# The final norm of a three-block network: its sums made beside the last product, its last multiplications shared by two engines

## The chip, the cores and the metric

The kernel runs on one core of one Trainium2 chip. The metric is the device time of one execution in microseconds (us), lower is better; the time before is the median of three runs. The engines of the core are TensorE (PE in the profile, its weight loads PEld), VectorE (DVE), ScalarE (ACT), GpSimd (POOL) and SyncE (SP), which here only issues DMAs.

## The reference

Three blocks of different kinds (an RWKV and differential-attention block, a convolution and sparse-attention block, a linear-attention block) work one after the other on a residual stream `x` of 512 tokens by 1024 features. Only the end of the third block is touched by the change:

```python
def rmsnorm_3(x, g):
    x32 = x.astype(jnp.float32)
    y = x32 * lax.rsqrt(jnp.mean(x32 * x32, axis=-1, keepdims=True) + EPS)
    return (y * g.astype(jnp.float32)).astype(x.dtype)

def third_block(...):
    for l in range(DEPTH):
        u = rmsnorm_3(x, g_norm_mix[l])
        x = x + mixer_block(u, ...).astype(x.dtype)
        u = rmsnorm_3(x, g_norm_mlp[l])
        x = x + jnp.square(jax.nn.relu(u @ w_mlp_in[l])) @ w_mlp_out[l]
    return rmsnorm_3(x, g_final)
```

The last line is the final norm: each token's 1024 features are squared and summed, and every feature is multiplied by the reciprocal root of the mean and by its own weight `g_final`.

## The kernel before

Data lies with the features on the 128 partitions: `x` is 8 tiles of 128 features by 512 tokens, tile k holding features 128k to 128k + 127. A sum over features is therefore a matmul with a matrix of ones.

The dense products run in `chain`, one stage that works through a list of `Job`s. A job is a weight matrix cut into slabs of 8 x 128 x 128 weights. SP loads slab s into a ring of four buffers (`wbuf`, the first of which is called `ahead`), ACT copies it to a rounded high part (`whi`, L256), DVE subtracts to get the low part (`wlo`, L338), and PE multiplies high by high, low by high and high by low (L240), 24 matmuls of 128x512 a slab. ACT and DVE make the parts three slabs ahead of PE; a buffer of `whi` is free again when PE has done the slab four before (`w_used`). When a tile of the output is complete, its `evict` takes it out of PSUM. In the last job of the third block, the second half of `mlp_out`, a tile takes two slabs, and the eviction is one DVE addition `x<-acc,x` (L404): 8 tiles, 16 slabs.

The order on each engine is written out by hand in the blocks of `chain`: for slab s first the parts of slab s + 3, then statistics, then the eviction. Some jobs already carry a `Fold`: there the squares (ACT, L271) and their running sum (DVE, L372) of the norm that follows are made right after each tile's eviction, and after the job PE needs one matmul with the ones (`stat`, L216), DVE the mean plus epsilon (L350), ACT the root (L267) and DVE the reciprocal (L359). The last job has no `Fold`.

After `chain` has closed, with a barrier of all engines, a stage of its own, `rmsnorm`, makes the final norm: SP loads the weights (L514), ACT squares the 8 tiles (L529), PE sums them with 8 matmuls into one PSUM bank (L542; float32, so the trace shows 16), DVE the mean (L554), ACT the root (L531), DVE the reciprocal (L556), then 8 multiplications by weight and reciprocal at once (L559), each released to SP, which stores the tile (L521) and at the end waits for all stores. The semaphores of a stage are cleared at its end.

Of the kernel before, what the change touches and what calls it, by code (L numbers as in the profile page):

```python
# [58 lines left out]
class Job:  # L59
# [15 lines left out]
    def makes_pair(self, n):  # L75
        return self.kind in ("join", "relu2") or (self.kind == "ffn" and n % 2 == 1) or self.fold is not None
# [15 lines left out]
class Fold:  # L92
# [3 lines left out]
    def __init__(self, pair, cols, eps, inner=None, eps_inner=None):  # L96
        self.pair, self.cols, self.eps, self.inner, self.eps_inner = pair, cols, eps, inner, eps_inner

# [5 lines left out]
def chain(nc, ones, jobs, T, norm, pending=None, ring=4, side=None, loads=(), taps=None, restore=None, ahead=None,  # L104
# [39 lines left out]
    for s, f in folds:  # L144
        per = 7 * (2 if f.inner is not None else 1)
        sum_no[s], summed_total = (summed_total, summed_total + per), summed_total + per
        fold_job[s] = slabs[s - 1][0]
    two_norms = any(f.inner is not None for f in stat_at.values())
# [11 lines left out]
    with stage(nc) as s_:  # L160
# [18 lines left out]

        first_in = wbuf[0]  # L180
# [10 lines left out]
        with nc.Block() as block:  # L191
            @block.sync
            def _(sp):
# [11 lines left out]
                if following is not None:  # L205
                    sp.wait_ge(lo_ready, (S - 1) // ring * ring + 1)
                    n = following.shape[3] // -(-following.shape[3] // 8)
                    sp.dma_start(first_in[:, 0:n, :], following[0, 0, :, 0:n, :]).then_inc(ahead[1], 16)

            @block.tensor  # L210
            def _(pe):
# [9 lines left out]
                for s, (j, n, i) in enumerate(slabs):  # L221
# [23 lines left out]
                    if side is not None:  # L245
                        side.pe(pe, s, stat)

            @block.scalar
            def _(act):
# [19 lines left out]
                def folded(f, n, x):  # L269
                    copy(f.pair[0][n], x, ACT.Copy, scale=f.cols[:, n:n + 1]).then_inc(hi_done, 1)  # L270
# [57 lines left out]
                if loads:  # L328
                    act.wait_ge(arrived, 16 * len(loads))

            @block.vector
            def _(dve):
# [28 lines left out]
                def folded(f, n, x, last):  # L361
                    no = sum_no[last][0]
                    dve.wait_ge(hi_done, part["made", fold_job[last], n])
# [78 lines left out]
                for s, (j, n, i) in enumerate(slabs):  # L442
# [12 lines left out]
                    if side is not None:  # L455
                        side.dve(dve, s)

# [31 lines left out]


def rmsnorm(nc, ones, x, weight, out, T, eps, src=None, dst=None):

    pair = isinstance(out, tuple)
    K = x.shape[1]
    nh, th = halves(T)
    with stage(nc) as s:
        w = s.sb("norm_w", [P, K])  # L500
        sq = s.sb("squares", [P, K, T])
        rstd = s.sb("rstd", [P, T])
        acc = s.ps("sum_squares", [P, nh, BANK])
        loaded, squared, summed = s.sem("loaded"), s.sem("squared"), s.sem("summed")
        mean_ready, root_ready, order, stored = s.sem("mean_ready"), s.sem("root_ready"), s.sem("order"), s.sem("stored")
        ready, hi_ready = s.sem("normed"), s.sem("hi_ready")

        whole = sq if pair else out
        acc_v = acc[:, :, 0:th]
        rstd_v = rstd[:].rearrange("p (h t) -> p h t", h=nh)  # L510
        with nc.Block() as block:  # L511
            @block.sync
            def _(sp):
                sp.dma_start(w[:], weight).then_inc(loaded, 16)  # L514
                if src is not None:
                    for k in range(K):
                        sp.dma_start(x[:, k, :], src[:, k, :]).then_inc(loaded, 16)
                if dst is not None:
                    for k in range(K):
                        sp.wait_ge(ready, k + 1)  # L520
                        sp.dma_start(dst[:, k, :], out[:, k, :]).then_inc(stored, 16)  # L521
                    sp.wait_ge(stored, 16 * K)

            @block.scalar
            def _(act):
                for k in range(K):
                    if src is not None and k == 0:
                        act.wait_ge(loaded, 16 + 16 * K)
                    nc.scalar.activation(sq[:, k, :], x[:, k, :], ACT.Square).then_inc(squared, 1)  # L529
                act.wait_ge(mean_ready, 1)  # L530
                nc.scalar.activation(rstd[:], rstd[:], ACT.Sqrt).then_inc(root_ready, 1)  # L531
                if pair:
                    for k in range(K):
                        act.wait_ge(ready, k + 1)
                        nc.scalar.activation(out[0][:, k, :], whole[:, k, :], ACT.Copy).then_inc(hi_ready, 1)

            @block.tensor
            def _(pe):
                for k in range(K):
                    pe.wait_ge(squared, k + 1)  # L540
                    for h in range(nh):
                        mm = nc.tensor.matmul(acc[:, h, 0:th], ones[:], sq[:, k, h * th:(h + 1) * th],  # L542
                                              start=(k == 0), stop=(k == K - 1))
                mm.then_inc(summed, 1)

            @block.vector
            def _(dve):
                def low_part(k):
                    dve.wait_ge(hi_ready, k + 1)
                    nc.vector.tensor_tensor(out[1][:, k, :], whole[:, k, :], out[0][:, k, :].bitcast(F32), ALU.subtract)  # L550

                chain = Chain(dve, order)
                dve.wait_ge(summed, 1)
# [3157 lines left out]
```

## Time and profile before

| | us |
|---|---|
| median of 3 runs | 3673.82 |
| the three runs | 3668.71 to 3677.48 |
| span of the profiled execution | 3676.3 |
| PE busy in it | 3363.3 (91%) |
| DVE, ACT, POOL busy | 2025.1, 1230.3, 203.8 |
| HBM read, written | 264.22 MB, 19.89 MB |

The profile lists for one execution what every engine did and when. The span runs from the first to the last instruction, and all times of the trace are counted from its start. "Idle before" is the time an engine stood still before an instruction, with the instruction that ended the wait. PEclk is the clock that TensorE was granted, as a share of full speed.

### The profile page before, as it was taken

The page shows a single profiled execution, that of the slowest core. Times are in us where ns is not written, and L with a number is a line of the kernel's source. Part 1 is how long each engine was busy: PE and PEld are TensorE (multiplying, and loading weights), DVE is VectorE, ACT ScalarE, POOL GpSimd, SP SyncE. Part 2 cuts the span into 40 slices and gives each one's busy share as a digit, 9 for nine tenths or more (in the row PEclk, how much of TensorE's full clock was granted, in tenths as well). Part 3 has the DMA queues.
Part 4 walks back from the last instruction along what each step waited for, and adds up shares of the span by engine and source line. Part 5 has one row for each costly group of instructions (what it writes and reads, how often), then busy time and mean ns, then how long its engine had stood idle before and what let it go on. Part 6 is the DMA issues. An engine that isn't in the chain of part 4 may idle for free. (4 is left out here: it accounts for less than half of the span.)

```text
span 3676.3 us, 57266 instructions
## 1 busy us (share of the span) xinstructions
PE 3363.3 (91%) x24193; PEld 2748.5 (75%) x24193; DVE 2025.1 (55%) x3289; ACT 1230.3 (33%) x2142; POOL 203.8 (6%) x171
## 2 busy tenths in 40 slices
PE   7978999988999999888999998978699889999998
PEld 6868888956888888656677776866578587878886
DVE  4875654565355344577546776356736545464342
ACT  4542332254334233214433222234412234233231
POOL 2213220010000000000000000000100020000000
PEclk9989998988999999989999999989799889999999
DMA  4431103201322222520122222312022003233231
GB/s 147 156 124 48 48 19 116 69 1 52 97 93 92 98 92 80 145 72 13 47 75 92 86 86 93 99 59 93 13 92 95 1 2 109 78 106 98 93 97 58
DMA packets 99462, 287.84 MB, mean 78 GB/s; under 512 B 19738, under 2 KB 23962, under 8 KB 97160
## 3 DMA queue, kind: packets, MB, share of 16 engines
q1 hardware_dynamic: 93104, 269.43, 22.6%
q10 hardware_dynamic: 6104, 14.75, 1.6%
q8 instruction: 193, 3.16, 0.4%
q14 instruction: 61, 0.50, 0.0%
HBM read 264.22 MB, written 19.89 MB: 77 GB/s over the span
## 5 line engine op out<-in xcount | busy, mean ns | idle before, releaser
L240 PE MATMUL acc<-h_hi,whi 128*128 128x512 f32 x1992 | 800.5, 402 | 65.4 <-DVE wlo L432 43.0
L240 PE MATMUL acc<-h_hi,wlo 128*128 128x512 f32 x1992 | 791.1, 397 | 0.0
L240 PE MATMUL acc<-h_lo,whi 128*128 128x512 f32 x1928 | 770.0, 399 | 0.0
L240 PEld LDWEIGHTS acc<-h_hi,whi 128*128 128x128 f32 x1992 | 379.1, 190 | 176.0 <-DVE wlo L432 45.3
L338 DVE TENSOR_TENSOR wlo<-wbuf,whi 128x1024 fp32r<-128x1024 f32 (+3 forms) x277 | 318.6, 1150 | 272.9 <-ACT whi L256 270.5
L240 PEld LDWEIGHTS acc<-h_hi,wlo 128*128 128x128 f32 x1992 | 379.3, 190 | 87.8
L240 PEld LDWEIGHTS acc<-h_lo,whi 128*128 128x128 f32 x1928 | 366.8, 190 | 86.2 <-issue 2.9
L256 ACT ACTIVATE whi<-wbuf 128x1024 fp32r<-128x1024 f32 (+3 forms) x277 | 274.5, 991 | 347.4 <-PE acc L240 318.3
L240 PE MATMUL acc<-arena_round,whi 128*128 128x512 f32 x736 | 236.6, 392 | 4.8 <-DVE arena_round L398 4.8
L338 DVE TENSOR_TENSOR wlo<-ahead,whi 128x1024 fp32r<-128x1024 f32 (+3 forms) x132 | 152.3, 1154 | 140.9 <-ACT whi L256 140.2
L256 ACT ACTIVATE whi<-ahead 128x1024 fp32r<-128x1024 f32 (+3 forms) x132 | 131.4, 995 | 174.7 <-PE acc L240 168.3
L240 PEld LDWEIGHTS acc<-arena_round,whi 128*128 128x128 f32 x736 | 139.2, 189 | 35.0 <-DVE arena_round L398 5.6
L240 PE MATMUL acc<-arena_round,wlo 128*128 128x512 f32 x416 | 162.8, 391 | 0.0
L240 PE MATMUL acc<-gates_round,whi 128*128 128x512 f32 x384 | 141.2, 395 | 3.0 <-DVE gates_round L398 1.8
L404 DVE TENSOR_TENSOR x<-acc,x 128x512 f32<-128x512 f32 x64 | 44.3, 692 | 178.1 <-PE acc L240 178.1
L670 PE MATMUL acc<-h_hi,whi 128*128 128x264 f32 x432 | 127.4, 295 | 7.5 <-POOL wlo L658 7.5
L240 PE MATMUL acc<-gates_round,wlo 128*128 128x512 f32 x320 | 125.5, 392 | 0.0
L670 PE MATMUL acc<-h_hi,wlo 128*128 128x264 f32 x432 | 123.5, 286 | 0.0
L670 PE MATMUL acc<-h_lo,whi 128*128 128x264 f32 x432 | 123.5, 286 | 0.0
L1430 PE MATMUL acc<-h_hi,whi 128*128 128x264 f32 x384 | 115.9, 302 | 1.1 <-DVE wlo L1468 1.1
L289 ACT ACTIVATE val<-tmp 128x512 f32<-128x512 f32 x64 | 40.5, 633 | 216.7 <-DVE tmp L400 216.7
L1430 PE MATMUL acc<-h_lo,whi 128*128 128x264 f32 x384 | 109.6, 285 | 0.0
(748 smaller groups left out, 6265.7 us busy)
## 6 DMA issues: line engine op xcount, KB each, us to landing
wbuf<-in_mlp_out SPq DMA_DIRECT2D x46, 512.0 KB, 3.3
wbuf<-in_mlp_in SPq DMA_DIRECT2D x45, 512.0 KB, 3.3
wbuf<-in_w_gates SPq DMA_DIRECT2D x38, 512.0 KB, 3.4
wbuf<-in_ffn_up SPq DMA_DIRECT2D x29, 512.0 KB, 3.3
wbuf<-in_w_qkv SPq DMA_DIRECT2D x23, 512.0 KB, 3.4
rwkv_factors<-factors SPq DMA_DIRECT2D x8, 1320.0 KB, 4.6
ahead<-in_mlp_in SPq DMA_DIRECT2D x19, 512.0 KB, 3.4
wbuf<-in_w_rwkv SPq DMA_DIRECT2D x18, 512.0 KB, 5.7
```

What stands on the lines that cost most here:

```text
L240: mm = nc.tensor.matmul(acc[t % NB][:, 0:T], wt[s % ring][:, k - a, :], xt, start=(kx == 0 and q == 0), stop=(kx == job.K - 1 and q == 2))
L256: copy(whi[s % ring][:, 0:size(s), :], wbuf[s % ring][:, 0:size(s), :], ACT.Copy).then_inc(hi_ready, 1)
L289: copy(val[t % 2][:], tmp[t % 2][:], ACT.Square)
L338: TT(wlo[s % ring][:, 0:size(s), :], wbuf[s % ring][:, 0:size(s), :], whi[s % ring][:, 0:size(s), :].bitcast(F32), ALU.subtract).then_inc( ...
L404: TT(job.dst[n], ps, job.other[n], ALU.add).then_inc(evicted_d, 1)
L670: mm = nc.tensor.matmul(acc[n % 2][:, hf, 0:H], wt[n % R][:, kx, :], xt[:, kx, at], start=(kx == 0 and q == 0), stop=(kx == 7 and q == 2))
L1430: mm = nc.tensor.matmul(acc[n % NB][:, h, 0:H], wt[n % R][:, k, :], xt[:, k, h * H:(h + 1) * H], start=(k == 0 and q == 0), stop=(k == 7 a ...
```

## The change

The stage `rmsnorm` and its call are dropped. The last job gets a new kind of fold, `Ending`, that holds the columns of the final weight (a ninth column block of the resident tile `norms`, which grows from 256 to 288 bytes a partition), epsilon and the output.

- While the last product runs, ACT squares each tile of `x` after its eviction and then multiplies the tile in place by its weight; DVE adds the square to the running sum.
- After the last tile PE makes one matmul of the sum with the ones, DVE the mean plus epsilon, ACT the root, DVE the reciprocal, all inside `chain`.
- The multiplications by the reciprocal are now plain products of two tiles. DVE makes tiles 0, 1, 2, 4, 5 and 7, GpSimd tiles 3 and 6, each after waiting for the reciprocal.
- SP stores the tiles in the order 0 to 7, each after the product that makes it.

```diff
--- before.py
+++ after.py
@@ -73,7 +73,7 @@
         return self.kind in ("copy", "sigmoid") and not self.scaled
 
     def makes_pair(self, n):
-        return self.kind in ("join", "relu2") or (self.kind == "ffn" and n % 2 == 1) or self.fold is not None
+        return self.kind in ("join", "relu2") or (self.kind == "ffn" and n % 2 == 1) or isinstance(self.fold, Fold)
 
 
 class Ahead:
@@ -95,6 +95,13 @@
 
     def __init__(self, pair, cols, eps, inner=None, eps_inner=None):
         self.pair, self.cols, self.eps, self.inner, self.eps_inner = pair, cols, eps, inner, eps_inner
+
+
+class Ending:
+
+
+    def __init__(self, cols, eps, dst):
+        self.cols, self.eps, self.dst, self.inner = cols, eps, dst, None
 
 
 def tile_list(ap):
@@ -145,6 +152,9 @@
         per = 7 * (2 if f.inner is not None else 1)
         sum_no[s], summed_total = (summed_total, summed_total + per), summed_total + per
         fold_job[s] = slabs[s - 1][0]
+    ending = next((f for _, f in folds if isinstance(f, Ending)), None)
+    ends_on = jobs[-1].dst
+    by_dve_last = (0, 1, 2, 4, 5, 7)
     two_norms = any(f.inner is not None for f in stat_at.values())
 
     def first_tile(j):
@@ -177,6 +187,8 @@
             s_.sem(n) for n in ("stat_ready", "var_ready", "root_ready", "scale_ready", "inverse_ready", "inner_ready", "order", "padded",
                                 "conv_done", "gelu_done", "arrived"))
 
+        scaled, last_normed, last_stored = (s_.sem(n) for n in ("scaled", "last_normed", "last_stored")) if ending else (None,) * 3
+        last_pool = s_.sem("last_pool") if ending else None
         first_in = wbuf[0]
         if side is not None:
             side.prepare(s_, evicted_d)
@@ -206,6 +218,22 @@
                     sp.wait_ge(lo_ready, (S - 1) // ring * ring + 1)
                     n = following.shape[3] // -(-following.shape[3] // 8)
                     sp.dma_start(first_in[:, 0:n, :], following[0, 0, :, 0:n, :]).then_inc(ahead[1], 16)
+                if ending is not None:
+                    for k in range(8):
+                        if k in by_dve_last:
+                            sp.wait_ge(last_normed, by_dve_last.index(k) + 1)
+                        else:
+                            sp.wait_ge(last_pool, 1 if k == 3 else 2)
+                        sp.dma_start(ending.dst[:, k, :], ends_on[k]).then_inc(last_stored, 16)
+                    sp.wait_ge(last_stored, 16 * 8)
+
+            @block.gpsimd
+            def _(pool):
+                if ending is not None:
+                    pool.wait_ge(scale_ready, len(stat_at) + 1)
+                    pool.wait_ge(scaled, 8)
+                    for k in (3, 6):
+                        nc.gpsimd.tensor_tensor(ends_on[k], ends_on[k], scale[:], ALU.mult).then_inc(last_pool, 1)
 
             @block.tensor
             def _(pe):
@@ -244,6 +272,9 @@
                         statistics(s)
                     if side is not None:
                         side.pe(pe, s, stat)
+                if ending is not None:
+                    pe.wait_ge(summed, sum_no[S][1])
+                    nc.tensor.matmul(stat[0][:, 0:T], ones[:], sums[0][:], start=True, stop=True).then_inc(stat_ready, 1)
 
             @block.scalar
             def _(act):
@@ -267,6 +298,10 @@
                     copy(scale[:], scale[:], ACT.Sqrt).then_inc(root_ready, 1)
 
                 def folded(f, n, x):
+                    if f is ending:
+                        copy(sums[0][:] if n == 0 else sqx[n % 2][:], x, ACT.Square).then_inc(sq_done, 1)
+                        copy(x, x, ACT.Copy, scale=f.cols[:, n:n + 1]).then_inc(scaled, 1)
+                        return
                     copy(f.pair[0][n], x, ACT.Copy, scale=f.cols[:, n:n + 1]).then_inc(hi_done, 1)
                     copy(sums[0][:] if n == 0 else sqx[0][:], x, ACT.Square).then_inc(sq_done, 1)
                     if f.inner is not None:
@@ -327,6 +362,9 @@
                         side.act(act, s)
                 if loads:
                     act.wait_ge(arrived, 16 * len(loads))
+                if ending is not None:
+                    act.wait_ge(var_ready, len(stat_at) + 1)
+                    copy(scale[:], scale[:], ACT.Sqrt).then_inc(root_ready, 1)
 
             @block.vector
             def _(dve):
@@ -360,6 +398,13 @@
 
                 def folded(f, n, x, last):
                     no = sum_no[last][0]
+                    if f is ending:
+                        dve.wait_ge(sq_done, no * 8 // 7 + n + 1)
+                        if n > 0:
+                            if n > 1:
+                                dve.wait_ge(summed, no + n - 1)
+                            TT(sums[0][:], sums[0][:], sqx[n % 2][:], ALU.add).then_inc(summed, 1)
+                        return
                     dve.wait_ge(hi_done, part["made", fold_job[last], n])
                     STT(out=f.pair[1][n], in0=x, scalar=f.cols[:, n:n + 1], in1=f.pair[0][n].bitcast(F32), op0=ALU.mult,
                         op1=ALU.subtract).then_inc(lo_done, 1)
@@ -454,6 +499,16 @@
                         STT(out=x[s - 1], in0=x[s - 1], scalar=cols[:, s - 1:s], in1=inner_rstd[:], op0=ALU.mult, op1=ALU.mult)
                     if side is not None:
                         side.dve(dve, s)
+                if ending is not None:
+                    no = len(stat_at) + 1
+                    dve.wait_ge(stat_ready, no)
+                    TS(scale[:], stat[0][:, 0:T], 1.0 / (8 * P), ending.eps, ALU.mult, ALU.add).then_inc(var_ready, 1)
+                    dve.wait_ge(root_ready, no)
+                    nc.vector.reciprocal(scale[:], scale[:]).then_inc(scale_ready, 1)
+                    dve.wait_ge(scale_ready, no)
+                    dve.wait_ge(scaled, 8)
+                    for k in by_dve_last:
+                        TT(ends_on[k], ends_on[k], scale[:], ALU.mult).then_inc(last_normed, 1)
 
 
 def settle(eng, sem):
@@ -486,82 +541,6 @@
                 for dst, src in pairs:
                     sp.dma_start(dst, src).then_inc(arrived, 16)
                 sp.wait_ge(arrived, 16 * len(pairs))
-
-
-def rmsnorm(nc, ones, x, weight, out, T, eps, src=None, dst=None):
...
-                    nc.scalar.activation(sq[:, k, :], x[:, k, :], ACT.Square).then_inc(squared, 1)
...
-                        mm = nc.tensor.matmul(acc[:, h, 0:th], ones[:], sq[:, k, h * th:(h + 1) * th],
...
-                    nc.vector.scalar_tensor_tensor(out=whole[:, k, :], in0=x[:, k, :], scalar=w[:, k:k + 1], in1=rstd[:],
...
 T1 = 528
@@ -3510,12 +3489,10 @@
                 Job(a["up_3"][1], pairs[1], "sum", dst=arena[8:16], gate=arena[8:16], other=arena[16:24], raw=parts[1]),
                 Job(a["up_3"][0], pairs[0], "join", dst=joined, gate=arena[0:8], other=arena[8:16], raw=parts[0]),
                 Job(a["w_out_3"], joined, "add", dst=xs, other=xs, source=3, fold=Fold(now, norms[:, MLP[1], :], 1e-6))]
-        jobs += mlp_jobs(xs, now, hidden, a["mlp_in_3"], a["mlp_out_3"], None)
+        jobs += mlp_jobs(xs, now, hidden, a["mlp_in_3"], a["mlp_out_3"], Ending(norms[:, LAST, :], 1e-6, out))
         for j, source in ((5, 4), (6, 5), (8, 7)):
             jobs[j].source = source
         chain(nc, ones, jobs, T2, norm, ahead=ahead.take(), side=HeadNorm(nc, ones, o_m, a["norm_mlstm_3"], norm[1][1], norm[2]))
-    rmsnorm(nc, ones_ident["ones"], x, a["norm_final_3"], x, T2, 1e-6, dst=out)
-
 
 def program(nc, a, out):
 
@@ -3540,7 +3517,7 @@
 
 
 
-INNER, OUTER, MLP, FFN, PLE = (0, 2), (1, 3), (4, 5), 6, 7
+INNER, OUTER, MLP, FFN, PLE, LAST = (0, 2), (1, 3), (4, 5), 6, 7, 8
 CONSTANTS = {
     0: ["ones", "ident", "norms"],
     1: ["blk64", "mean64", "chunk_start1", "causal_pair", "level_pair", "eye_pair", "mask128", "rope_cos", "rope_sin", "rope_swap"],
@@ -3688,7 +3665,7 @@
         a[name] = column(i[key])
     a["norms"] = np.stack([column(v) for v in (
         i["final_norm_w"], i["norm_mix_2"], i["norm_final_2"], i["g_norm_mix_3"], i["norm_mlp_w"][0], i["g_norm_mlp_3"], i["norm_ffn_2"],
-        i["norm_ple_2"])], 1)
+        i["norm_ple_2"], i["g_final_3"])], 1)
     a["up_3"] = np.stack([tiles(i["w_up_3"][0, n], 4) for n in range(3)])
     a["w_out_3"], a["mlp_in_3"], a["mlp_out_3"] = tiles(i["w_out_3"][0]), tiles(i["w_mlp_in_3"][0]), tiles(i["w_mlp_out_3"][0])
     return a
```

On DVE, at the end of the program. Before (`rstd` is the reciprocal root, `squares` and `sum_squares` belong to the dropped stage):

```order
L338 TENSOR_TENSOR wlo<-wbuf,whi 128x1024
L404 TENSOR_TENSOR x<-acc,x 128x512 x2
L191 UNCONDITIONAL_BRANCH
L546 UNCONDITIONAL_BRANCH
L554 TENSOR_SCALAR rstd<-sum_squares 128x512
L556 RECIPROCAL rstd<-rstd 128x512
L559 SCALAR_TENSOR_TENSOR x<-x,norm_w,rstd 128x512 x8
```

After, on the same engine at the same place:

```order
L376 TENSOR_TENSOR wlo<-wbuf,whi 128x1024
L449 TENSOR_TENSOR x<-acc,x 128x512
L406 TENSOR_TENSOR sums<-sums,sqx 128x512
L449 TENSOR_TENSOR x<-acc,x 128x512
L406 TENSOR_TENSOR sums<-sums,sqx 128x512
L505 TENSOR_SCALAR scale<-stat 128x512
L507 RECIPROCAL scale<-scale 128x512
L511 TENSOR_TENSOR x<-x,scale 128x512 x6
```

Behind each eviction now stands an addition to the sum, the branch into a stage of its own is gone, and six products of two tiles stand where eight products with weight and reciprocal stood.

On ACT, at the end of the program. Before:

```order
L256 ACTIVATE whi<-ahead 128x1024
L256 ACTIVATE whi<-wbuf 128x1024 x3
L191 UNCONDITIONAL_BRANCH
L524 UNCONDITIONAL_BRANCH
L529 ACTIVATE squares<-x 128x512 x8
L531 ACTIVATE rstd<-rstd 128x512
```

After:

```order
L287 ACTIVATE whi<-wbuf 128x1024 x2
L302 ACTIVATE sqx<-x 128x512
L303 ACTIVATE x<-x,norms 128x512
L287 ACTIVATE whi<-wbuf 128x1024
L302 ACTIVATE sqx<-x 128x512
L303 ACTIVATE x<-x,norms 128x512
L302 ACTIVATE sqx<-x 128x512
L303 ACTIVATE x<-x,norms 128x512
L367 ACTIVATE scale<-scale 128x512
```

The squares moved from behind the barrier to between the parts of the last slabs, each followed by the multiplication by the weight; no load of a function table stands in either stretch. On GpSimd, whose last work before was hundreds of us earlier, the products are new, the last but one row of this piece (before, only the first three of its rows stood there):

```order
L3195 TENSOR_TENSOR sums<-inner_rstd,dec 128x512
L2995 UNCONDITIONAL_BRANCH
L41 ISA
L230 UNCONDITIONAL_BRANCH
L236 TENSOR_TENSOR x<-x,scale 128x512 x2
L203 UNCONDITIONAL_BRANCH
```

These are the products for tiles 3 and 6, beside the six of DVE.

## Rows read from the trace of the kernel before

**Rows 1.** The page, busy time of each engine in the whole span.

```profile
PE 3363.3 (91%) x24193; PEld 2748.5 (75%) x24193; DVE 2025.1 (55%) x3289; ACT 1230.3 (33%) x2142; POOL 203.8 (6%) x171
```

**Rows 2.** Chain that ended last, in time order: start us, length us, what.

```profile
3653.58 0.64 ACT squares L529
...
3654.26 8.85 PE sum_squares L542 x16
...
3663.13 0.70 DVE rstd L554
...
3663.86 0.64 ACT rstd L531
...
3664.52 3.36 DVE rstd L556
...
3667.91 0.75 DVE x L559
```

**Rows 3.** Timeline of DVE, last eviction: start, length, line, operation, [idle before].

```profile
3651.94 0.69 DVE L404 TENSOR_TENSOR x<-acc,x 128x512 f32<-128x512 f32 x1 [10.19 <-PE acc L240]
```

**Rows 4.** Timeline around a `Fold` in the same chain, DVE and PE.

```profile
3301.11 0.68 DVE L372 TENSOR_TENSOR sums<-sums,sqx 128x512 f32<-128x512 f32 x1
...
3304.09 0.42 PEld L216 LDWEIGHTS stat<-sums,ones 128*128 128x128 f32 x2
3304.32 1.02 PE L216 MATMUL stat<-sums,ones 128*128 128x512 f32 x2
```

**Rows 5.** Busy time by stretch: A:B, us, each engine, PEclk, DMA share, GB/s.

```profile
3260.00:3303.00 43.00, 43.00 (x185) 35.32 (x184) 24.73 (x30) 18.54 (x25) 0.00 (x0) 0.97 0.29 98
...
3600.00:3651.90 51.90, 51.90 (x229) 42.63 (x228) 10.12 (x10) 6.37 (x6) 0.00 (x0) 1.00 0.09 31
```

**Rows 6.** The same view, stretches of PE's idle time and the sums.

```profile
3651.90:3654.20 2.30, 0.00 (x1) 0.00 (x0) 0.69 (x1) 0.62 (x2) 0.00 (x0) 1.00 0.00 0
...
3655.30:3658.70 3.40, 3.40 (x6) 1.34 (x5) 0.00 (x0) 2.54 (x5) 0.00 (x0) 0.50 0.00 0
```

**Rows 7.** Timeline of DVE early in the program, two places.

```profile
103.43 2.96 DVE L798 SCALAR_TENSOR_TENSOR k<-dif,vec,rkv 128x528 f32<-128x528 f32 x1
...
198.29 0.77 DVE L798 SCALAR_TENSOR_TENSOR k<-dif,vec,rkv 128x528 f32<-128x528 f32 x1
199.09 2.51 DVE L805 TENSOR_SCALAR kk<-k,vec 128x528 f32<-128x528 f32 x1
```

**Rows 8.** Timeline of GpSimd at the same two places.

```profile
103.44 2.38 POOL L658 TENSOR_TENSOR wlo<-wbuf,whi 128x1024 fp32r<-128x1024 f32 x1 [4.33 <-ACT whi L735]
...
198.37 2.93 POOL L658 TENSOR_TENSOR wlo<-wbuf,whi 128x1024 fp32r<-128x1024 f32 x1 [4.32 <-ACT whi L735]
```

**Rows 9.** Groups of GpSimd's operations by form: count, busy us, mean ns, idle before.

```profile
L1730 POOL TENSOR_TENSOR rot<-p,rope_cos 128x512 f32<-128x512 f32 x8 | 10.2, 1273 | 278.9 <-POOLq L42 195.2 <-PE ps_s L1626 83.8
...
L3216 POOL TENSOR_TENSOR sums<-inner_rstd,dec 128x512 f32<-128x512 f32 x4 | 4.2, 1049 | 8.8 <-DVE inner_rstd L3294 8.8
```

**Rows 10.** Timeline of the last stage: multiplications and store issues.

```profile
3667.91 5.39 DVE L559 SCALAR_TENSOR_TENSOR x<-x,norm_w,rstd 128x512 f32<-128x512 f32 x8
3668.68 4.97 SPq L521 DMA_DIRECT2D out_features<-x  x8
```

**Rows 11.** Busy time by stretch, columns as in Rows 5, while the stores run.

```profile
3669.00:3670.00 1.00, 0.00 (x0) 0.00 (x0) 1.00 (x3) 0.00 (x0) 0.00 (x0) 0.50 0.47 176
3670.00:3671.00 1.00, 0.00 (x0) 0.00 (x0) 1.00 (x2) 0.00 (x0) 0.00 (x0) 0.50 1.04 393
...
3674.00:3675.00 1.00, 0.00 (x0) 0.00 (x0) 0.00 (x0) 0.00 (x0) 0.00 (x0) 0.50 0.92 352
3675.00:3676.30 1.30, 0.00 (x0) 0.00 (x0) 0.00 (x0) 0.00 (x0) 0.00 (x0) 0.50 0.00 0
```

**Rows 12.** Waits by pair over the whole span: us in total, times, longest.

```profile
ACT whi L735 <- DMA first<-in_w_rwkv: 9.0, 5, 2.5
...
ACT whi L303 <- DMA ahead<-in_w_gates: 4.7, 1, 4.7
```

More of the change, by code:

```diff
@@ L488, in _ @@
                 sp.wait_ge(arrived, 16 * len(pairs))
-def rmsnorm(nc, ones, x, weight, out, T, eps, src=None, dst=None):
[L496 to L528, printed above, removed]
-                    nc.scalar.activation(sq[:, k, :], x[:, k, :], ACT.Square).then_inc(squared, 1)
[L530 to L541, printed above, removed]
-                        mm = nc.tensor.matmul(acc[:, h, 0:th], ones[:], sq[:, k, h * th:(h + 1) * th],
[L543 to L553, printed above, removed]
-                nc.vector.tensor_scalar(rstd_v, acc_v, 1.0 / (K * P), eps, ALU.mult, ALU.add).then_inc(mean_ready, 1)
-                dve.wait_ge(root_ready, 1)
-                chain(nc.vector.reciprocal(rstd[:], rstd[:]))
-                dve.wait_ge(loaded, 16 if src is None else 16 + 16 * K)
-                for k in range(K):
-                    nc.vector.scalar_tensor_tensor(out=whole[:, k, :], in0=x[:, k, :], scalar=w[:, k:k + 1], in1=rstd[:],
-                                                   op0=ALU.mult, op1=ALU.mult).then_inc(ready, 1)
-                    if pair and k > 0:
-                        low_part(k - 1)
-                if pair:
-                    low_part(K - 1)
```

## The prediction

> **What bounds the kernel now.** The change touches the last 110 us of the program and one constant at its start, so I read the end of the trace first. The busy shares say that TensorE bounds the whole, with 91% of the span [rows 1]. The stretches say it more sharply for the last product: PE is busy 51.90 of 51.90 us up to its last matmul, at full granted clock, while DVE is busy 10.12 and ACT 6.37 us [rows 5]. What follows is the opposite. The chain of waits from there on is one string of single instructions that hand over to each other [rows 2]. It begins with the last addition `x<-acc,x`, which ends at 3651.94 + 0.69 = 3652.63 [rows 3], and its links are: 0.95 us until the new stage's first square starts at 3653.58, the squares and the 16 matmul passes that follow each other to 3663.11, the mean 0.70, the root 0.64, the reciprocal 3.36, and the first multiplication at 3667.91. The string from the last addition to that point is 3667.91 - 3652.63 = 15.28 us long. Then eight multiplications (5.39 us, to 3673.30) release eight stores of 256 KB, the first issued at 3668.68 [rows 10], and the span ends at 3676.3. So there are two pieces to cost: the string of 15.28 us, and the 8.39 us from the first multiplication to the end.
>
> **Work moved under the product: nothing.** Per tile ACT gains a square and a scaled copy, two instructions of 0.64 us or a little less, 8 x 1.28 = 10 us in 87 us of product; DVE gains seven additions of 0.68 us [rows 2, 4]. What could it delay? ACT waits for the eviction before it makes the next high part, so that part, which stands at the end of the slab before, starts some 0.69 + 1.28 = 2 us later, and the low part on DVE behind it. But both are needed only three slabs later, and the last product spends 10.9 us on two slabs (the additions before it stand that far apart: the last one's idle time is 10.19 us, and 0.69 us busy [rows 3]), so 16 us of slack cover 2. The same pattern already stands in the job `w_out_3`, whose tiles come twice as often and whose fold is longer: in the window 3260 to 3303 PE was busy 43.00 of 43.00 us beside 24.73 us of DVE and 18.54 of ACT [rows 5]. If that cover failed, each late slab would show as idle time of PE. No SP transfer is delayed, since SP waits only for low parts. The dropped load of `norm_w` was on no one's path.
>
> **The string of 15.28 us becomes 7.5.** After the last addition there now stand one square 0.64, one addition to the sum 0.68, the two passes of one matmul, the mean 0.70, the root 0.64 and the reciprocal 3.36 [rows 2, 4]. The matmul, from its first weight load at 3304.09 to the end of its passes at 3304.32 + 1.02 = 3305.34, is 1.25 us [rows 4]. The sum is 7.27 us. The seven handovers cost about 0.03 us each (the mean ends at 3663.83, the root starts at 3663.86 [rows 2]), 0.25 in all: 7.52 us. **Saved: 15.28 - 7.52 = 7.76 us.** One term has two ends. PE stands idle here for 2 us before the matmul, as it did before the first of the old sums (2.30 us without PE work); from 3655.30 to 3658.70 the granted clock was 0.50, which is the 1.2 GHz level, before it came back to 1.00 [rows 6]. At the time of the new matmul, 2.1 to 3.4 us after the last slab, the clock was still 1.00 in that execution, so I take 1.25 us; if the fall comes earlier, both passes run at half the clock and it is up to 0.85 us more.
>
> **The multiplications: do two engines share them?** Split without friction, DVE would make six at a pitch of 5.39 / 8 = 0.67 us, 4.05 us, and GpSimd two. The prices on GpSimd are 1.27 us (two tiles read) and 1.05 us (a tile times a repeated column) [rows 9]; I take 1.27, the form being that of the product here, so 2.5 us beside DVE. But the trace shows what happens when the two work at once. At 103.44 GpSimd starts a subtraction of 2.38 us; DVE's operation of two SBUF tiles starts at 103.43 and takes 2.96 us, where the same line takes 0.77 at 198.29: it ends 0.57 us after GpSimd. At 198.37 GpSimd starts while DVE holds on until 199.06; GpSimd then takes 2.93 instead of 2.38, and DVE's next, started at 199.09, takes 2.51 and ends 0.30 us after GpSimd's [rows 7, 8]. So the two exclude each other, each waits for the other's running instruction, and the waiting GpSimd gets in between two of DVE's. Here both operands of both engines lie in SBUF. The Trainium skill says the same of it (SBUF — State Buffer, the section on its two separate sides): a DVE operation with two SBUF inputs and a GpSimd operation that reads SBUF share a pair of ports as an exclusive lock. The trace agrees, as just shown. Then the eight products take turns. Counting from the reciprocal: tile 0 to 0.69; tile 3 on GpSimd to 1.96; tile 1 to 2.53 (0.57 behind GpSimd); tile 6 to 3.80; tile 2 to 4.37; tiles 4, 5, 7 to 6.38 at 0.67 each. That is 1.0 us longer than the 5.39 of now.
>
> **The stores make it dearer.** Once running, they fill the DMA engines: share 1.04 from 3670 on, 0.92 up to 3675, then nothing [rows 11]. 2.1 MB in about 5.4 us is 0.67 us a tile, just DVE's pace today. They begin some 0.8 us after the first issue (0.47 of the slice 3669 to 3670 is busy [rows 11]) and end at 7.0 us after the first multiplication began. So no split can bring the end closer by making products faster: a frictionless one gains under 0.1 us. A delayed one loses, because SP issues in the order 0 to 7 and tile 2 waits: tile 0 issued at 0.71, tile 1 at 2.55, tile 2 at 4.39, then 3 to 7 to 6.43 (an issue is about 0.35 us). Tiles 2 to 7 are six transfers that start at 4.39 + 0.8 = 5.19 and need 6 x 0.67 = 4.03: the last ends at 9.22 instead of 6.97. **Lost: 2.25 us.** If GpSimd keeps its turn for both products, tile 1 is issued at 3.8 and seven transfers end at 9.3 (lost 2.4); if DVE keeps its turn through all six, tile 3 is issued at 5.3 and tile 7 at 7.0, and the end is 9.5 (lost 2.5). At GpSimd's cheaper price the loss is 1.8. From the last transfer to the end of the span nothing changes: the wait, the barrier, the clearing.
>
> **Sum.** -7.76 + 2.25 = -5.5 us. Span 3676.3 - 5.5 = 3670.8; the profiled execution lies 2.5 us over the median and inside the spread of the three runs, and I carry the difference over: 3673.82 - 5.5 = **3668.3 us**, 0.15% faster. What a measurement of this kernel can tell from no change is about 0.2%, 7.3 us. Own range of this case, with the clock's 0.85 and the prices above: 5.9 to 4.4 us faster.
>
> **Rivals.** *No exclusion at the end* (the products are short and DVE wins nothing by waiting): then the stores set the pace as now and the gain is 7.76 + 0.06 = 7.8 us, 3666.0, just over 0.2%. Against it: at both places of rows 7 and 8 an instruction is held, three in all, among them one of DVE that reads a single tile. *The cover fails*: the later high and low parts reach PE late and part of the gain comes back as gaps in PE between 3565 and 3652; at 2 us a tile on eight tiles it would be 16 us, 3684. It decides only where the delay of 2 us passes the slack of 16, which rows 5 speak against. *The tiles lie elsewhere*, the slower case: `norms` grows by 32 bytes, and every tile allocated behind it starts 32 bytes later, for the whole program. If transfers became longer by it, it would cost where an engine waits for a DMA: the eight pairs in the list of waits, from 9.0 down to 4.7 us, sum to 56 us [rows 12]. To turn 5.5 us of gain into 7.3 of loss, those waits would have to grow by 12.8 us, 23%, which is where this case decides: 3681.1. Against it: `x` is already read at a start of 64 bytes plus k times 2,112, off any round grid for most tiles, and its stores still keep up with DVE's 0.67 us [rows 10, 11]. The Trainium skill gives a rule for it (DMA: Bandwidth & Descriptors, How a descriptor splits into AXI transactions): a transfer that does not start on a multiple of 256 bytes needs an extra transaction, nine instead of eight for a run of 2,048 bytes; by that page's figure the estimate would be an eighth of 56 us, 7 us, and 3675.3. No row here shows such a difference.
>
> **Chances.** The forecast (exclusion, parts covered) 0.78. No exclusion 0.12. The cover fails 0.03. Tiles elsewhere with a visible cost 0.07, a third of it past the point for slower. The runs of before lie 8.8 us apart, so a median of a few moves by 2 or 3 us: of the forecast, a quarter is measured as faster by over 0.2%, and hardly any as slower; of no exclusion, over half. Together: faster 0.27, within 0.2% 0.67, slower 0.06. The range for 8 in 10, with that spread about the forecast and the no-exclusion case inside: 3662.5 to 3674.5.
>
> **What would show it.** Right: PE without a gap up to its last matmul; from the last addition's end to the first product of `x` and `scale` 7.5 us; GpSimd's products or DVE's next to them drawn out (a DVE row of about 1.9 us in the group whose others take 0.69), the last product ending 6.4 us after the reciprocal, stores issued with holes behind tiles 0 and 1, and the span's end about 10.6 us after the first product. Wrong: all DVE products at 0.67 and the end at 8.4 us (no exclusion); gaps in PE inside the last product; the program's earlier stages a few us longer (the shift); a weight load and matmul of `stat` of 2 us (the clock).

## The result and the profile after

The changed kernel took 3668.19 us, the median of 20 runs (3661.17 to 3678.92), against 3674.82 us for the kernel before in its 20 runs beside it (3667.85 to 3682.47). The ratio is 0.9982, 95% interval 0.9975 to 0.9989, that is 4.0 to 9.2 us faster. The forecast was 3668.3 us; against 3673.82, a gain of 5.5 us. The measured gain, 0.18%, stays below the 0.2% from which the forecast would have called the kernel faster.

The page of the profiled execution after, span and busy time (answers to [rows 1]):

```profile
span 3664.6 us, 57236 instructions
...
PE 3351.7 (91%) x24179; PEld 2743.7 (75%) x24179; DVE 2037.6 (56%) x3294; ACT 1235.5 (34%) x2150; POOL 206.7 (6%) x173
```

The end of the chain that ended last, in order of time (start us, length us, what; answers to [rows 2, 3]):

```profile
3645.93 0.70 DVE x L449
3646.65 0.64 ACT sqx L302
3647.32 0.70 DVE sums L406
3648.06 1.14 PE stat L277 x2
3649.23 0.70 DVE scale L505
3649.95 0.64 ACT scale L367
3650.61 3.37 DVE scale L507
3654.00 0.69 DVE x L511
3654.69 1.67 DVEq L203
3656.36 3.48 DVE x L511 x4
```

`DVEq` is DVE's queue: for these 1.67 us DVE's second product was waiting or at work behind its first.

The last addition ends at 3645.93 + 0.69 = 3646.62 and the first product starts at 3654.00: 7.38 us where 15.28 us were before.

The timeline of the last stretch, DVE, GpSimd and the store issues (answers to [rows 10]):

```profile
3654.00 5.84 DVE L511 TENSOR_TENSOR x<-x,scale 128x512 f32<-128x512 f32 x6
3654.04 3.44 POOL L236 TENSOR_TENSOR x<-x,scale 128x512 f32<-128x512 f32 x2 [637.38 <-DVE scale L507]
3654.72 6.43 SPq L227 DMA_DIRECT2D out_features<-x  x8
```

From the first product to the end of the span it is 3664.6 - 3654.00 = 10.6 us, where 8.4 us were before. Narrow windows on the same timeline show single instructions of the two engines:

```profile
3656.28 1.75 DVE L511 TENSOR_TENSOR x<-x,scale 128x512 f32<-128x512 f32 x1
...
3654.04 1.77 POOL L236 TENSOR_TENSOR x<-x,scale 128x512 f32<-128x512 f32 x1 [637.38 <-DVE scale L507]
...
3655.77 1.71 POOL L236 TENSOR_TENSOR x<-x,scale 128x512 f32<-128x512 f32 x1
...
3658.06 0.33 SPq L227 DMA_DIRECT2D out_features<-x  x1
```

GpSimd starts 0.04 us behind DVE's first product and must wait for its end at 3654.69; its own end at 3655.81 lets DVE finish its second at 3656.36, and so on: DVE, GpSimd, DVE, GpSimd, and then four products of DVE. Six products take 5.84 us. The last line is the issue of tile 2's store, 4.06 us after the first product began. The occupation of the DMA engines between 3654 and 3665, 40 slices of 0.275 us in tenths, shows what this does to the stores:

```profile
DMA  0000029920019920019999999999999980000000
```

The first tile goes out alone, then a hole, the second, a hole, and only from 3658.9 on six tiles without a gap until 3663.0.

The last product in two stretches, up to its last matmul, and the stretch that holds the single matmul (A:B, us, each engine's busy time, PEclk, DMA share, GB/s; answer to [rows 5, 6]):

```profile
3560.00:3600.00 40.00, 40.00 (x178) 33.10 (x177) 13.96 (x14) 12.49 (x16) 0.00 (x0) 1.00 0.26 92
3600.00:3645.90 45.90, 45.89 (x203) 37.68 (x201) 11.66 (x13) 9.95 (x13) 0.00 (x0) 1.00 0.07 24
...
3648.00:3649.20 1.20, 1.12 (x2) 0.30 (x2) 0.01 (x1) 0.00 (x0) 0.00 (x0) 1.00 0.00 0
```

PE has no visible gap (0.01 us in 85.90) beside the moved squares and additions, and the matmul ran at full granted clock.

The two profiled spans differ by 11.7 us, and only 23.67 - 17.98 = 5.69 us of that lie behind the last addition (before: 3676.3 - 3652.63; after: 3664.6 - 3646.62). The other 6.0 us lie ahead of it, where the programs differ only in the places of the tiles and in the work moved under the last product, beside which PE has no gap. They are taken up with the experiments.

### The profile page after: what moved, and what is told of

Read it like the earlier page. It is cut to its first block and busy times, and to the rows that moved or that the text cites. A ratio compares the mean times of both kernels' runs of the same rounds, so it can differ in the third digit from the quotient of the medians.

```text
span 3664.6 us, 57236 instructions
## 1 busy us (share of the span) xinstructions
PE 3351.7 (91%) x24179; PEld 2743.7 (75%) x24179; DVE 2037.6 (56%) x3294; ACT 1235.5 (34%) x2150; POOL 206.7 (6%) x173
```

## The experiments

The kernels of one group ran on the same chip beside the kernel before. "String" is the time from the end of the last addition `x<-acc,x` to the first product with the reciprocal, "end" the time from that product's start to the end of the span, both from the profile. Ratios are to the kernel before of the same group.

| kernel | string us | end us | ratio | 95% interval |
|---|---|---|---|---|
| before | 15.28 | 8.4 | 1 | |
| changed | 7.38 | 10.6 | 0.9982 | 0.9975 to 0.9989 |
| after_again | 7.39 | 10.6 | 0.9993 | 0.9982 to 1.0005 |
| all_dve | 7.38 | 8.6 | 0.9978 | 0.9968 to 0.9988 |
| split_alone | 15.27 | 10.3 | 1.0015 | 1.0003 to 1.0027 |
| shift_alone | 15.27 | 8.5 | 1.0006 | 0.9998 to 1.0015 |
| stores_free | 7.38 | 8.6 | 0.9974 | 0.9962 to 0.9986 |
| heavy_cover | 7.38 | 10.6 | 0.9976 | 0.9965 to 0.9986 |
| last_square_pe | 6.72 | 8.6 | 0.9962 | 0.9948 to 0.9976 |
| shorter_tail | 3.34 | 8.7 | 0.9959 | 0.9944 to 0.9974 |
| pool_after_dve | 7.38 | 11.0 | one run | |
| after_third | 7.38 | 10.6 | 0.9980 | 0.9969 to 0.9991 |
| shorter_tail_again | 3.34 | 8.6 | 0.9970 | 0.9959 to 0.9981 |

**The split taken away.** All eight products on DVE:

```diff
-    by_dve_last = (0, 1, 2, 4, 5, 7)
+    by_dve_last = tuple(range(8))
...
-                    for k in (3, 6):
-                        nc.gpsimd.tensor_tensor(ends_on[k], ends_on[k], scale[:], ALU.mult).then_inc(last_pool, 1)
+                pass
```

> The changed kernel with all eight last products on DVE and none on GpSimd. Theory (the two engines exclude each other, and the stores need 0.67 us a tile in any case): the eight products take 8 x 0.67 = 5.4 us instead of 5.84, the stores start without holes, and from the first product to the end of the span it is 8.4 us instead of 10.6. So 2.2 us faster than the changed kernel and 7.7 us faster than before, ratio to before about 0.9979. Rival (the split is worth something, the holes in the stores have another cause): the end comes no earlier or later than 10.6 us after the first product.

The products took less than expected, 4.91 us at a pitch of 0.60, and the end 8.6 us, 2.0 less than in the changed kernel. The interval of the ratio holds the expected 0.9979. The ratio of its partner on the chip, the changed kernel once more, is higher, though the two intervals overlap a little; the 2.0 us are read from the traces:

> The changed kernel unaltered, as the partner of the three others on this chip. Exclusion theory: from the end of the last addition to the first product of x and scale 7.4 us, from there to the end of the span 10.6 us, GpSimd's two products 1.7 to 1.8 us each and two of DVE's about 1.75 us, as in its first profile. Ratio to the kernel before 0.998 to 0.9985, 5 to 7 us. If the first measurement was luck of the run, the ratio is nearer to 1.

Timeline of all_dve, last stretch:

```profile
3660.45 4.91 DVE L507 TENSOR_TENSOR x<-x,scale 128x512 f32<-128x512 f32 x8
3661.17 4.54 SPq L227 DMA_DIRECT2D out_features<-x  x8
```

Eight products on one engine end sooner (4.91 us) than six beside two on the other (5.84 us).

**The split alone.** The kernel before, with the last multiplications divided as in the change, its own stage kept:

```diff
                     nc.scalar.activation(sq[:, k, :], x[:, k, :], ACT.Square).then_inc(squared, 1)
+                if dst is not None:
+                    act.wait_ge(loaded, 16)
+                    for k in range(K):
+                        nc.scalar.activation(x[:, k, :], x[:, k, :], ACT.Copy, scale=w[:, k:k + 1]).then_inc(weighted, 1)
...
+                    for k in (3, 6):
+                        nc.gpsimd.tensor_tensor(x[:, k, :], x[:, k, :], rstd[:], ALU.mult).then_inc(by_pool, 1)
...
+                    for k in on_dve:
+                        nc.vector.tensor_tensor(x[:, k, :], x[:, k, :], rstd[:], ALU.mult).then_inc(ready, 1)
```

> The kernel before with its own last stage kept, and in it only the last multiplications changed: ACT multiplies the tiles by the weight after the squares, hidden behind the sums on PE, then DVE makes the products of tiles 0, 1, 2, 4, 5, 7 and GpSimd those of 3 and 6. Theory: the exclusion is a property of the two engines and the string in front of the products stays 15.3 us, so from the first product to the end of the span 10.6 us instead of 8.4, and the kernel is 2.2 us slower than before, ratio 1.0006. Rival (the split itself helps and only its neighbourhood in the changed kernel spoils it): 8.4 us or less, 7 us in the best case.

Timeline of split_alone, last stretch:

```profile
3674.66 5.83 DVE L578 TENSOR_TENSOR x<-x,rstd 128x512 f32<-128x512 f32 x6
3674.70 3.44 POOL L535 TENSOR_TENSOR x<-x,rstd 128x512 f32<-128x512 f32 x2 [645.14 <-DVE rstd L574]
```

The same 5.83 and 3.44 us in other surroundings, the string unchanged, and the ratio is 1.0015 (1.0006 expected, inside the interval): the only kernel whose interval lies wholly above 1. The end was 10.3 us, 1.95 more than before.

**The two engines made to work one after the other.**

```diff
                     pool.wait_ge(scaled, 8)
+                    pool.wait_ge(last_normed, 6)
```

> The changed kernel, but GpSimd begins its two products only when DVE has made all of its six, so that the two never work at once; nothing else changes, the stores keep their order 0 to 7. Theory (exclusion): DVE's six products take 6 x 0.60 + 0.08 = 3.7 us with none drawn out, GpSimd's two about 1.1 us each, and tiles 3 to 7 are stored late, so the end comes 9.5 to 10.5 us after the first product, no better than 10.6 by much. Rival (DVE's long products have another cause than GpSimd): two of them still take 1.75 us.

Its timeline:

```profile
3655.34 3.70 DVE L512 TENSOR_TENSOR x<-x,scale 128x512 f32<-128x512 f32 x6
3656.06 6.85 SPq L227 DMA_DIRECT2D out_features<-x  x8
3659.22 2.48 POOL L237 TENSOR_TENSOR x<-x,scale 128x512 f32<-128x512 f32 x2 [641.23 <-DVEq L203]
```

No product of DVE is drawn out any more, six take 3.70 us, and GpSimd's take 1.26 us each. So what drew two of DVE's products out to 1.75 us was the wait for GpSimd. The end, 11.0 us, was later than the 9.5 to 10.5 expected. GpSimd began 0.2 us behind DVE's last product, and its first took 1.26 us where 1.1 had been reckoned, so tile 3 was issued at 5.2 us after the first product. From there it is the stores' pace: 0.8 us to the first transfer, five transfers in 3.4 us, and 1.5 us to the end of the span.

**What the stores allow.** As all_dve, but seven of the eight products left out, so that all stores may go at once:

```diff
-                    for k in by_dve_last:
+                    for k in (0,):
...
-                        if k in by_dve_last:
-                            sp.wait_ge(last_normed, by_dve_last.index(k) + 1)
-                        else:
-                            sp.wait_ge(last_pool, 1 if k == 3 else 2)
+                        sp.wait_ge(last_normed, 1)
```

> As all_dve, but DVE makes only the product of tile 0, and the stores of all eight tiles wait for that one alone; the products of tiles 1 to 7 with the reciprocal are left out. Theory (the stores need 0.67 us a tile whatever the engines do): from the first product to the end of the span still 8.4 to 8.6 us as in all_dve, although the multiplying takes 0.7 us instead of 4.9. Rival (the end follows the last product): 8.6 - 4.2 = 4.4 us.

Timeline of stores_free from the product on, and the occupation of its DMA engines between 3650 and 3664 (0.35 us a slice):

```profile
3654.56 0.69 DVE L504 TENSOR_TENSOR x<-x,scale 128x512 f32<-128x512 f32 x1
3655.28 4.48 SPq L224 DMA_DIRECT2D out_features<-x  x8
...
DMA  0000000000000000059999999999999992000000
GB/s 0 0 0 0 0 0 0 0 0 0 0 0 0 0 0 0 0 187 386 375 392 369 386 375 386 363 398 369 404 369 404 375 374 82 0 0 0 0 0 0
```

With 0.69 us of multiplying instead of 4.91 the end is the same 8.6 us, and the transfers fill 5.4 us at some 380 GB/s. The floor of this stretch is the stores, given that the first of them goes out behind the first product.

**The cover made heavier.**

```diff
+                        for spare in (*val, *tmp) if n < 7 else ():
+                            copy(spare[:], x, ACT.Square)
                         copy(sums[0][:] if n == 0 else sqx[n % 2][:], x, ACT.Square).then_inc(sq_done, 1)
```

> The changed kernel with the work hidden under the last product made heavier: beside each of the first seven tiles' squares ACT makes four more that nobody reads, 4 x 0.53 = 2.1 us a tile and 15 us in all. Theory (16 us of slack for each high part): PE stays without a gap up to its last matmul, and the ratio is that of the changed kernel, 0.998 to 0.999; from the end of the last addition on nothing changes, 7.4 and 10.6 us. Rival (the cover is thin): gaps on PE in the last product, up to 15 us, ratio up to 1.002.

Busy time of heavy_cover in the whole last product:

```profile
3565.00:3650.00 85.00, 85.00 (x376) 70.38 (x375) 25.61 (x27) 36.81 (x56) 0.00 (x0) 1.00 0.16 56
```

PE was busy 85.00 of 85.00 us beside 36.81 us of ACT. The ratio, 0.9976, is even below the expected band, but its interval reaches to 0.9986. Ahead of the next high part ACT and DVE now have about 4 us of new work instead of 2. The cover holds that; the rest of the 16 us of slack was not tried.

**The shift of the tiles alone.** The kernel before with the ninth block of columns in `norms` and nothing else:

```diff
-        i["norm_ple_2"])], 1)
+        i["norm_ple_2"], i["g_final_3"])], 1)
```

> The kernel before with nothing changed but the constant norms, which gets its ninth block of columns, so that every tile allocated behind it starts 32 bytes later. Theory: no change, ratio 1.0000 within the interval, and the last stretch from the end of the last addition to the end of the span 23.7 us as before. Rival (the places of the tiles matter; they explain that the first profile of the changed kernel reached its last matmul 6 us earlier than the profile of before): a ratio of about 0.9984 with 6 us gained ahead of the last product, or, the other way, a loss.

The ratio is 1.0006 with 1 in its interval, and the profile's last addition ended at 3651.56 + 0.69 = 3652.25, 0.4 us from the 3652.63 of before. No gain from the places is seen. A loss of up to 0.15% is not excluded; the 7 us that the prediction estimated for this rival would be 1.0019, outside the interval. A third set of runs of the changed kernel was made for the same question:

> The changed kernel unaltered once more, since its two ratios so far, 0.9982 and 0.9993, have intervals that barely meet. By the trace of its last stretch the gain is 23.7 - 18.0 = 5.7 us, 0.9984. If something ahead of the last product also became faster, the ratio would be lower than that in all three.

It gave 0.9980, the expected 0.9984 well inside. The three executions of the changed program that were profiled tell where 6 us ahead of the last product come from. Span and mean granted TensorE clock of changed, after_again and after_third:

```profile
core 0: 3664.6 us, clock 0.951
...
core 0: 3677.2 us, clock 0.948
...
core 0: 3668.9 us, clock 0.950
```

The same program ends 12.6 us later in one execution than in another, all of it ahead of the last addition (string and end are the same to 0.02 and 0.1 us), and its granted clock is lower where it is longer. How much of the 12.6 us that is can be added up from the stretches ahead of the last addition in which the trace shows a granted clock of 0.50: 344.7 us in changed, 368.6 us in after_again. Where PE is the bound, half of such time is lost, so 23.9 us more of it are 12.0 us by this estimate. The same sum settles the 6.0 us of the first pair: before had 355.0 us at 0.50, 10.3 more than changed, which is 5.2 of the 6.0 us. Taken off in this way (end of the last addition less half of the time at 0.50), before, shift_alone and split_alone come to 3475.1, 3473.1 and 3475.1 us, and changed, after_again and after_third to 3474.2, 3474.9 and 3476.9 us. So the 6.0 us come mainly from the granted clock of the two executions, and beyond the 4 us by which these sums differ among themselves neither the tiles' places nor the moved work shows ahead of the last addition. Why the clock differs from one execution to the next stays open.

**A shorter end.** Two further edits on top of all_dve. First the last square goes straight to PE, which has begun with the sum of the other seven:

```diff
-                    pe.wait_ge(summed, sum_no[S][1])
-                    nc.tensor.matmul(stat[0][:, 0:T], ones[:], sums[0][:], start=True, stop=True).then_inc(stat_ready, 1)
+                    pe.wait_ge(summed, sum_no[S][1] - 1)
+                    nc.tensor.matmul(stat[0][:, 0:T], ones[:], sums[0][:], start=True, stop=False)
+                    pe.wait_ge(sq_done, sum_no[S][0] * 8 // 7 + 8)
+                    nc.tensor.matmul(stat[0][:, 0:T], ones[:], sqx[1][:], start=False, stop=True).then_inc(stat_ready, 1)
...
-                        if n > 0:
+                        if 0 < n < 7:
```

> As all_dve, and the last tile's square no longer goes through DVE's addition: PE multiplies the sum of seven tiles with the ones while the last square is still being made, and then adds the last square in the same PSUM bank. Theory: from the end of the last addition to the first product 7.4 - 0.7 = 6.7 us, the rest as in all_dve, 8.6 us; 8.4 us faster than before, ratio about 0.9977. Rival (PE's first matmul comes late or at half the clock and the second queues behind it): 7.4 us or more.

The string was 6.72 us, as expected. The ratio, 0.9962, is lower than the 0.9977 of the trace, which lies just outside its interval (0.9948 to 0.9976). All four kernels of this group have ratios 0.0005 to 0.0015 below what their traces give, against the same runs of the kernel before; why was not found, and the traces are taken for the size of each gain. Second, ACT makes the inverse root at once and the reciprocal goes:

```diff
-                    copy(scale[:], scale[:], ACT.Sqrt).then_inc(root_ready, 1)
+                    copy(scale[:], scale[:], ACT.Abs_reciprocal_sqrt).then_inc(root_ready, 1)
...
-                    nc.vector.reciprocal(scale[:], scale[:]).then_inc(scale_ready, 1)
-                    dve.wait_ge(scale_ready, no)
```

> As last_square_pe, and ACT makes the inverse root in one instruction in place of the root on ACT and the reciprocal of 3.36 us on DVE; its function table is loaded behind the last scaled copy, before the mean is there. Theory: from the end of the last addition to the first product 6.7 - 3.4 = 3.3 us, from there to the end of the span 8.6 us; 23.7 - 11.9 = 11.8 us faster than before, ratio about 0.9968. Rival (the load of the table, 1.28 us, is not hidden): 4.6 us and 0.9971.

Timeline of shorter_tail behind the last addition:

```profile
3646.33 1.12 PE L275 MATMUL stat<-sqx,ones 128*128 128x512 f32 x2 [0.59 <-ACT sqx L300]
3646.91 1.28 ACT L365 ACT_TABLE_LOAD   x1
3647.56 0.69 DVE L503 TENSOR_SCALAR scale<-stat 128x512 f32<-128x512 f32 x1 [1.95 <-PE stat L275]
3648.29 0.63 ACT L365 ACTIVATE scale<-scale 128x512 f32<-128x512 f32 x1
3648.95 4.90 DVE L507 TENSOR_TENSOR x<-x,scale 128x512 f32<-128x512 f32 x8 [0.69 <-ACT scale L365]
```

The load of the function table ends at 3648.19, just before the mean at 3648.25: hidden by 0.06 us. The string is 3.34 us, and string and end together 12.0 us, against 23.7 before and 18.0 in the change. A second set of runs stood beside after_third:

> The kernel shorter_tail unaltered once more, beside the changed kernel on one chip. By the traces of the last stretch it is 18.0 - 12.0 = 6.0 us faster than the changed kernel and 11.7 us faster than before, ratio 0.9968. A ratio of 0.996 again would point to a gain outside the last stretch.

0.9970 against 0.9980 of the changed kernel on that chip: the order is the expected one, though the intervals overlap. The trace supports 11.7 us over the kernel before, 0.9968, and both intervals hold it. This version is faster than before in both sets; over the change the gain is shown by the traces, while the medians alone don't separate the two beyond doubt.

## Why the prediction was right

**Work moved under the product, forecast nothing: right.** PE was busy 45.89 of 45.90 us, and with 15 us more on ACT it still had no gap (heavy_cover).

**The string, forecast 7.52 us: measured 7.38.** The matmul took 1.14 us from its first weight load instead of 1.25 (its two weight loads 0.30 instead of 0.42); the rest agrees row by row. Seven handovers of 0.03 us are 0.21 and not 0.25, so the forecast's own terms sum to 7.48, and less the 0.11 of the matmul that is 7.37. The granted clock stood at 1.00 during the matmul, the end of the term that had been chosen.

**The exclusion, forecast as alternating turns: right in mechanism and order, its size somewhat too large.** The last product ended 5.84 us after the first began, against 6.38. Two terms were mis-sized: the pitch of DVE's plain products is 0.60 us, not the 0.67 taken from the products with a weight [rows 10], and a GpSimd product in its turn holds DVE for 1.1 us (3654.69 to 3655.81), not 1.27; alone it takes 1.26 (pool_after_dve), so some of it overlaps with the wait. split_alone shows the same numbers without any other part of the change, and pool_after_dve shows them vanish when the engines don't meet.

**The stores, forecast 2.25 us lost: measured 10.6 - 8.4 = 2.2.** This agreement is partly luck. The store of tile 2 was released at 4.06 us after the first product instead of 4.39, which by the forecast's own sum should have given 0.3 us less. But the six transfers began 0.84 us behind it and took 4.12 us instead of 4.03, and behind the last transfer the changed kernel needs longer: its transfers end at 3663.0 and the span at 3664.6, 1.6 us, where it was 1.4 before (3674.9 to 3676.3). The forecast's "nothing changes" behind the last transfer was wrong by that 0.2 us. It isn't the split that costs it: all_dve and stores_free, which end in `chain` too, have 1.6 us there, while split_alone and shift_alone, which kept the old stage, have 1.4, and split_alone lost 1.95 us with the same pattern of products. So the 0.2 us go with the end of `chain` in place of the end of `rmsnorm`; which part of it was not tried. That the stores are the floor is shown by stores_free.

How much the turns cost hangs on SP's fixed order too. GpSimd had tile 3 ready at 1.81 us after the first product and tile 6 at 3.48, and the stores of both waited for tile 2. An estimate from these rows (0.84 us from issue to transfer, 0.67 us a tile): stored as they become ready, in the order 0, 3, 1, 6, 2, 4, 5, 7, the last transfer would end at 7.7 us instead of 9.0, and 1.3 of the 2.2 us would be gone. No run tried it.

**Sum.** -7.90 + 2.2 = -5.7 us by the traces, against -5.5 forecast. That the absolute 3668.3 us were met to 0.1 us is luck: the kernel before measured 3674.82 and not 3673.82 beside the change, the medians moved by 6.6 us and not 5.5, and single runs lie 18 us apart. The change came out within 0.2%, the outcome to which the forecast gave 0.67, and the three ratios of the changed kernel, 0.9982, 0.9993 and 0.9980, lie around the 0.9984 that the trace gives.

**The rivals.** No exclusion: refuted by the two drawn-out products of DVE. Its price was right, though: all_dve, where the engines don't meet, is at 0.9978, and 7.8 us faster is 0.9979. The failing cover: refuted by PE without a gap. The shifted tiles: no cost found, ratio 1.0006 with an interval of 0.9998 to 1.0015; the point at which this rival would have decided, 12.8 us, is 1.0035.

## What to carry to other kernels

Before work of DVE is handed to GpSimd, look in the trace for instructions of the two that overlap and read their lengths: here the two products that GpSimd took over saved DVE 1.2 us and cost it 2.1 us of waiting. Before products in front of stores are made faster, set the stores' own pace beside them: 0.67 us a tile was the floor, and with it what counts is that no hole follows the first store; SP's fixed order makes a late tile a hole. A norm's sums belong beside the product that makes its input; the string that is left is a count of single instructions, and each of them (a reciprocal of 3.36 us, an addition of 0.7) is paid in full.

## What the runs showed of the hardware that was not expected

The issue of a store on SP took 0.33 us where the issues came 0.60 us apart or more (all_dve, before), and 0.43 to 0.65 us where one followed right behind the other: in stores_free eight issues took 4.48 us, with nothing to wait for. The plain product of two tiles of 128x512 has a pitch of 0.60 us on DVE (eight in 4.91), the one with a weight beside it 0.67 (eight in 5.39). Both engines' waits for each other are counted as busy time of the waiting instruction: six DVE products were 5.84 us "busy" of which 2.1 us were waiting, so a higher busy share of an engine is no proof of more work.
